# Recurrent stage: the sum of r times k moved into two 64x64 quadrants beside the variance product

## What is computed

```python
y = moveaxis(scan(step, S0, (r, w, k, v, kk, a)))            # the recurrence
mean = jnp.mean(y, axis=-1, keepdims=True)
var = jnp.mean(jnp.square(y - mean), axis=-1, keepdims=True)
y = (y - mean) * lax.rsqrt(var + GN_EPS)
y = y * gn_gain + gn_bias
y = y + jnp.sum(r * k * r_k, axis=-1, keepdims=True) * v     # the sum of r times k
y = y.reshape(bsz, seq, A_WIDTH).astype(dt) * jax.nn.silu(z)
```

## Time and profile before

| | |
|---|---|
| median of 3 runs | 2566.21 us (2562.79 to 2568.52) |
| profiled execution | 2567.88 us |
| its span on the core | 2566.1 us |
| mean granted clock | 0.998 |
| PE busy over the span | 2509.3 us, 98% |
| DVE, ACT, POOL busy | 54%, 31%, 46% |

### The profile page before, as it was taken

How to read it: one execution, slowest core, us unless ns; L and a number is a source line. 1 busy time by engine, 2 the same in 40 slices (tenths; PEclk the granted TensorE clock), 3 DMA queues, 4 the chain that set the end, 5 groups by cost and what they waited for, 6 DMA issues and landing times.

```text
span 2566.1 us, 52423 instructions
## 1 busy us (share of the span) xinstructions
PE 2509.3 (98%) x21640; PEld 2000.4 (78%) x21640; DVE 1382.1 (54%) x1496; ACT 804.2 (31%) x1187; POOL 1184.6 (46%) x1403
## 2 busy tenths in 40 slices
PE   8999999999999999999999999999999999999999
PEld 6777778888878888888888877777777777776877
DVE  7664431114676666652245675553647575654873
ACT  4433330002443333331013435554232323223241
POOL 7643324446676566565576651122422232323450
PEclk9999999999999999999999999999999999999999
DMA  3111001113222222273112220001111111114341
GB/s 141 42 34 34 26 26 49 49 49 115 107 74 90 74 82 90 76 267 115 49 49 82 82 74 18 16 16 68 44 37 55 40 56 39 39 64 165 140 139 58
DMA packets 46996, 184.25 MB, mean 72 GB/s; under 512 B 6257, under 2 KB 6769, under 8 KB 42609
## 3 DMA queue, kind: packets, MB, share of 16 engines
q1 hardware_dynamic: 30240, 106.01, 12.4%
q10 hardware_dynamic: 16592, 75.77, 7.7%
HBM read 145.06 MB, written 36.70 MB: 71 GB/s over the span
## 4 chain that ended last, share of the span: by engine, by line
PE 86%; DVE 7%; ACT 3%; issue 2%; DMA 1%; POOL 1%; ACTq 0%; POOLq 0%; DVEq 0%; SPq 0%
PE dps L336 36%; PE dps L354 14%; PE dps L1193 11%; PE aps L2519 6%; PE aps L1193 4%; PE aps L3389 2%; PE dps L697 2%; PE dps L688 1%; PE aps L675 1%; PE dps L1963 1%; PE aps L2055 1%; PE aps L2025 1%; PE dps L2076 1%; PE dps L2068 1%; DVE h_lo L404 1%
## 5 line engine op out<-in xcount | busy, mean ns | idle before, releaser
L3572 POOL TENSOR_TENSOR w_hi<-w_raw,one 128x256 fp32r<-128x256 f32 (+1 forms) x534 | 374.6, 731 | 1127.7 <-PE dps L336 514.0
L3577 POOL TENSOR_TENSOR w_lo<-w_raw,w_hi 128x256 fp32r<-128x256 f32 (+1 forms) x542 | 512.5, 975 | 13.3 <-ACT w_hi L1561 12.8
L336 PE MATMUL dps<-h_hi,w_hi 128*128 128x512 f32 x832 | 266.1, 395 | 12.8 <-POOL w_lo L3577 11.1
L1193 PE MATMUL dps<-op,ff_w 128*128 128x512 f32 x1122 | 270.1, 390 | 0.6 <-DVE op L1018 0.5
L336 PE MATMUL dps<-h_lo,w_hi 128*128 128x512 f32 x832 | 262.4, 390 | 0.0
L336 PE MATMUL dps<-h_hi,w_lo 128*128 128x512 f32 x832 | 262.3, 390 | 0.0
L1193 PEld LDWEIGHTS dps<-op,ff_w 128*128 128x128 f32 x1122 | 210.2, 188 | 46.3 <-DVE op L1018 2.1
L336 PEld LDWEIGHTS dps<-h_hi,w_hi 128*128 128x128 f32 x832 | 156.3, 189 | 50.7 <-POOL w_lo L3577 11.1
L336 PEld LDWEIGHTS dps<-h_lo,w_hi 128*128 128x128 f32 x832 | 156.9, 189 | 32.8
L336 PEld LDWEIGHTS dps<-h_hi,w_lo 128*128 128x128 f32 x832 | 156.7, 188 | 32.9
L336 PE MATMUL dps<-hid,w_hi 128*128 128x512 f32 x676 | 180.8, 389 | 1.1 <-DVEq L1460 1.1
(11 more groups left out here) (570 smaller groups left out, 4848.8 us busy)
## 6 DMA issues: line engine op xcount, KB each, us to landing
w_raw<-w_stream SPq DMA_DIRECT2D x192, 512.0 KB, 3.5
hid_t<-ff_up ACTq DMA_DIRECT2D x11, 1024.0 KB, 3.9
hid_raw<-hid_t ACTq DMA_DIRECT2D x22, 512.0 KB, 6.4
gates<-gate_out ACTq DMA_DIRECT2D x16, 512.0 KB, 3.3
gate_ring<-gates ACTq DMA_DIRECT2D x14, 512.0 KB, 4.8
x_res<-x_t ACTq DMA_DIRECT2D x2, 2048.0 KB, 7.8
x_res<-x_t ACTq DMA_DIRECT2D x4, 1024.0 KB, 6.0
x_t<-x_res ACTq DMA_DIRECT2D x4, 1024.0 KB, 4.1
```

The costliest lines, as they stand in the source:

```text
L336: mm = k.nc.tensor.matmul(k.dps[0:rows, pair, h * HALF:(h + 1) * HALF], w[:, slot, sub + t, 0:rows], x(t)[:, h * HALF:(h + 1) * HALF], sta ...
L1193: mm = k.nc.tensor.matmul(out, w[:, q, :], x, start=q == 0 and n == 0 and j not in (3, 5), stop=q == QUARTER - 1 and n == 2, skip_group_ch ...
L3572: g.tensor_tensor(k.w_hi[:, s, at], k.w_raw[:, s, at], ones, ALU.mult).then_inc(k.sem("w_hi_done"), 1)
L3577: return g.tensor_tensor(k.w_lo[:, s, at], k.w_raw[:, s, at], k.w_hi[:, s, at].bitcast(F32), ALU.subtract)
```

## The change

`rk` leaves level 4. At level 5, behind the wait for t5, one wide run of four 64x64 quadrant products of 512 columns takes the place of the variance product: for each head h, the variance from rows h to outputs h in bank 3, and `rk` from rows h to the other head's outputs in bank 2. The first half of the stage has no earlier half, so there only the two `rk` quadrants run. ScalarE gets a step `crossed`: two copies of 64x512 that put the halves of `rk` back in place in `rw_rk`, behind `std` and ahead of the `akv` copy. VectorE's multiplication by v moves from level 4 to behind the last level, ahead of the `rk_t` mask, and reads `rw_rk`. TensorE waits for the copy before it writes bank 2 again (w1 and rk_t). Level 4 now waits for the t4 mask. In the last half `back_load` moves from behind the `kq_tm` copy to behind the `w1` copy.

```diff
--- before.py
+++ after.py
@@ -281,6 +281,7 @@
         k.half[name] = k.half[room]
     for n, name in enumerate(("turn", "s", "y")):
         k.half[name] = k.at(f"rw_{name}", L + 2 * n * kb, [NC, HD])
+    k.rw_rk = k.at("rw_rk", L + 10 * kb, [HALF])
 
     k.back = [k.at(f"back{n}", at, [S]) for n, at in enumerate([X + 4 * n * kb for n in (0, 1, 2, 5, 6)] + [C, C + 4 * kb])]
     k.yb2_hi, k.yb2_lo, k.ya2_hi, k.ya2_lo = (k.at(name, H + 16 * n * kb, [PAIRS, S], F32R)
@@ -2283,10 +2284,10 @@
 EXPS = Steps("rw_exps", ["pc", "p", "q"])
 
 PRODUCTS = Steps("rw_product", ["lt", "lt_x", "l", "t1", "ak_t", "x1", "xt1", "t2", "v_tm", "x2", "xt2", "t3", "rb_t", "x3", "xt3",
-                                "t4", "kq_tm", "rk", "x4", "xt4", "kkp_tm", "t5", "bq_tm", "xt5", "akv", "u0", "w1", "rk_t", "m", "r", "y0"])
+                                "t4", "kq_tm", "x4", "xt4", "kkp_tm", "t5", "bq_tm", "rk", "xt5", "akv", "u0", "w1", "rk_t", "m", "r", "y0"])
 VALUES = Steps("rw_value", ["lt", "x_part", "x0", "xt_part", "xt0", "t1", "ak_t", "x1", "xt1", "t2", "x2", "xt2", "t3", "rb_t", "x3", "xt3",
-                            "t4", "rk", "x4", "xt4", "t5", "xt5", "rk_t", "m", "r", "s_in"])
-COPIES = Steps("rw_copy", ["v_tm", "kq_tm", "kkp_tm", "bq_tm", "akv", "u0", "w1"])
+                            "t4", "x4", "xt4", "t5", "xt5", "rk", "rk_t", "m", "r", "s_in"])
+COPIES = Steps("rw_copy", ["v_tm", "kq_tm", "kkp_tm", "bq_tm", "rk", "akv", "u0", "w1"])
 
 STATES = Steps("rw_state", [f"s{c}" for c in range(NC)])
 STATE_VALUES = Steps("rw_state_value", [f"s{c}" for c in range(NC)])
@@ -2296,7 +2297,7 @@
 Y_COPIES = Steps("rw_y_copy", ["y", "sq", "std"])
 
 BANK = {"lt": 0, "lt_x": 1, "l": 2, "t1": 0, "ak_t": 2, "x1": 1, "xt1": 0, "t2": 2, "v_tm": 1, "x2": 0, "xt2": 2, "t3": 1, "rb_t": 0,
-        "x3": 2, "xt3": 1, "t4": 0, "kq_tm": 2, "rk": 1, "x4": 1, "xt4": 0, "kkp_tm": 2, "t5": 1, "bq_tm": 2, "xt5": 0, "akv": 1, "rk_t": 2,
+        "x3": 2, "xt3": 1, "t4": 0, "kq_tm": 2, "rk": 2, "x4": 1, "xt4": 0, "kkp_tm": 2, "t5": 1, "bq_tm": 2, "xt5": 0, "akv": 1, "rk_t": 2,
         "u0": 0, "w1": 1, "y0": 2, "m": 0, "r": 1, "n": 3, "y": 3}
 
 
@@ -2598,12 +2599,8 @@
         b.then_inc(product, 1)
         if l < LEVELS:
             state(before, 2 * l - 1)
-        if l == 4:
-            u.wait(pe, VALUES, "xt3")
-            u.wait(pe, AHEAD, "rk")
-            k.nc.tensor.matmul(bank(k, "rk"), const(k, "headsum"), flat(made["rkv"]), start=True, stop=True).then_inc(product, 1)
         fill((count.late if l == LEVELS else count.level) - 1)
-        u.wait(pe, VALUES, "rk" if l == 4 else f"t{l}")
+        u.wait(pe, VALUES, f"t{l}")
         if l == 4:
             u.wait(pe, COPIES, "kq_tm")
             if before is not None:
@@ -2612,8 +2609,18 @@
             state_wait(before, 2 * l)
         else:
             u.wait(pe, COPIES, "bq_tm")
+            u.wait(pe, AHEAD, "rk")
             if before is not None:
-                rw_result_pe(k, pe, before, "var")
+                before.wait(pe, Y_COPIES, "sq")
+            for h in range(2):
+                if before is not None:
+                    var = k.nc.tensor.matmul(bank(k, "y")[HEADS[h]], const(k, "headsum")[HEADS[h], HEADS[h]], k.rw_out[HEADS[h], before.g, :],
+                                             start=True, stop=True, skip_group_check=True)
+                rk = k.nc.tensor.matmul(bank(k, "rk")[OTHER[h]], const(k, "headsum")[HEADS[h], HEADS[h]], flat(made["rkv"])[HEADS[h]],
+                                        start=True, stop=True, skip_group_check=True)
+            if before is not None:
+                var.then_inc(k.sem("rw_y_product"), 1)
+            rk.then_inc(product, 1)
         fill(1)
         if l < LEVELS:
             for c in range(NC):
@@ -2647,6 +2654,7 @@
         a = mul(bank(k, "u0"), SAME, c, other("xt"), other("akv"))
         mul(bank(k, "n"), HEADS, c, same("kq_tm"), same("v_tm"), start=c == 0, stop=False)
     a.then_inc(product, 1)
+    u.wait(pe, COPIES, "rk")
     for c in range(NC):
         a = mul(bank(k, "w1"), SAME, c, other("xt"), other("kkp_tm"))
         b = mul(bank(k, "rk_t"), SAME, c, channel("kq"), channel("rp"))
@@ -2909,10 +2917,6 @@
             rw_state_dve(k, dve, before, 2 * l - 1)
         elif before is not None:
             rw_result_dve(k, dve, before, "centred")
-        if l == 4:
-            rkv = flat(k.ahead["rkv"][u.g])
-            u.wait(dve, PRODUCTS, "rk")
-            v.tensor_tensor(rkv, bank(k, "rk"), k.rw_v[:, u.tokens], ALU.mult).then_inc(made, 1)
         steps(f"t{l}")
         for n, out in (("x", "xm"), ("xt", "xt")):
             if (n, l) != ("x", LEVELS):
@@ -2923,6 +2927,8 @@
         if l < 4:
             rw_state_dve(k, dve, before, 2 * l)
         steps(f"x{l}")
+    u.wait(dve, COPIES, "rk")
+    v.tensor_tensor(flat(k.ahead["rkv"][u.g]), k.rw_rk[:, :], k.rw_v[:, u.tokens], ALU.mult).then_inc(made, 1)
     u.wait(dve, PRODUCTS, "rk_t")
     mask("arkt", "rk_t", "incl_t").then_inc(made, 1)
     steps("ends")
@@ -3088,6 +3094,12 @@
         if u is not None:
             rw_result_act(k, act, u, step)
 
+    def crossed(u):
+        u.wait(act, PRODUCTS, "rk")
+        for to, src in zip(SAME, OTHER):
+            copied = a.activation(k.rw_rk[to, :], bank(k, "rk")[src], ACT.Copy)
+        copied.then_inc(k.sem("rw_copy"), 1)
+
     def spill(u):
         if u is not None:
             rw_spill(k, act, u, branches)
@@ -3103,6 +3115,7 @@
     copy(first, "bq_tm")
     result(prior[1], "sq")
     result(prior[1], "std")
+    crossed(first)
     copy(first, "akv")
     copy(first, "u0", -1.0)
     copy(first, "w1", -1.0)
@@ -3134,6 +3147,7 @@
         result(first, "sq")
         rw_shift_act(k, act, "r", i + 1, spilled)
         result(first, "std")
+        crossed(last)
         copy(last, "akv")
         copy(last, "u0", -1.0)
         copy(last, "w1", -1.0)
@@ -3144,15 +3158,16 @@
         spill(prior[1])
         gate(LAST_GATES[i][0], f"v{i}")
         copy(last, "kq_tm")
-        back_load(k, act, last, branches)
         copy(last, "kkp_tm")
         copy(last, "bq_tm")
         result(first, "sq")
         result(first, "std")
+        crossed(last)
         copy(last, "akv")
         gate(LAST_GATES[i][1], f"v{i}")
         copy(last, "u0", -1.0)
         copy(last, "w1", -1.0)
+        back_load(k, act, last, branches)
         result(last, "y")
         act.wait_ge(k.sem("gate_spilled"), 16 * (LAST_GATES[PAIRS - 1][1] + 1))
         for g in range(2):
```

## The result

The changed kernel takes 2570.39 us in the median (20 runs, 2568.74 to 2574.33), against 2566.19 us (20 runs) for the kernel before on the same chip: ratio 1.0019, 95% interval 1.0013 to 1.0025. It is 4.2 us slower where 3.0 us less was forecast: a miss of 7.2 us, outside the range. Against the bound of 0.2% the time counts as no change (it would begin at 2571.3), but the interval excludes a gain.

A forecast was written before the change was run, and what follows sets the result against it. The recurrent stage was taken as bound by TensorE's instruction list; seven halves at -3.4 us together and +0.4 for the first gave -3.0, other terms costing 0, so 2566.21 became 2563.2 us, range 2559.5 to 2567.5.

The forecast's parts named there:

- the price of the edit: TensorE, eight halves: rk removed saves 0.86 us each, wide run adds 0.38 in seven, 1.24 in the first; total -3.0 us.
- The wide run: TensorE at level 5: four quadrant products take 1.07 us, 1.79 us from filler to the first 64x64 matmul after.
- the two bunches that were named: Level 5: the wide run's eight matmuls start in two bunches of four, some 0.43 to 0.53 us apart.
- the two rivals on the array: Wide run: quadrants exclude each other on a bank, 2570.1 us, chance 0.06; all four run in a row, 2582.1, chance 0.02.
- levels and copies: Level 4's wait for the t4 mask, ScalarE's two added copies and VectorE's moved multiplication: each covered, cost 0.
- the issue waits: TensorE in the recurrent stage: three waits with no releaser, 2.5 us together, carried unchanged in the sum.
- The sum: TensorE's terms in the stage: -3.4 us for seven halves, +0.4 for the first, in all -3.0 us.
- the rival that named them: TensorE's issue waits, 2.5 us, may go, or the wide run is entered free: 2560.7 us or lower, chance 0.12.
- the seven DMA issues: Last half, back_load on ScalarE: moved issues take 3.38 us with 1.9 us of room, cost 0.
- the gate tile's landing: First gate tile, queued behind the branch loads: lands at 2351.6 to 2351.9 us, room 0.6 us or more, cost 0.
- a cover is lost: Gate tile lands 1 to 4 us late, or the akv copy is awaited: +1 to +4, 2564 to 2567 us, chance 0.12.

The follow-up runs named there:

- 8: The changed kernel run again unaltered, on the chip of the runs with waits at the head: 2571.09 us, ratio 1.0023 to the kernel before.
- 5: The changed kernel with 160 waits on an already set semaphore at the head of TensorE's program, shifting the stage by 80 instructions: 2563.63 us, ratio 0.9990.
- 3: The kernel before with eight dummy transposes (64 TensorE instructions) ahead of the stage's first product: 2570.61 us, ratio 1.0021.
- experiment 1: The kernel before with only the seven branch loads moved behind the w1 copy of the last half: 2567.84 us, ratio 1.0008.
- 9: The changed kernel with 244 waits on a set semaphore at the head of TensorE's program, a shift of 122 instructions: 2566.51 us, ratio 1.0002.
- 10: The changed kernel with 312 waits on a set semaphore at the head of TensorE's program, a shift of 156 instructions: 2567.94 us, ratio 1.0010.
- 4: The changed kernel with ten dummy transposes ahead of the stage's first product, a shift of 80 instructions: 2562.74 us, ratio 0.9993.
- experiment 2: The changed kernel with the branch loads issued later, behind the loads of the first two gate tiles: 2566.23 us, ratio 1.0006.

## Why the prediction was wrong, point by point

**Right: the price of the edit.** Level 4 (TensorE timeline of after, columns as in the earlier trace rows):

```profile
1977.79 0.73 PE L355 MATMUL dps<-h_hi,w_lo 128*128 128x512 f32 x2
1978.35 0.62 PE L355 MATMUL dps<-h_hi,w_hi 128*128 128x512 f32 x2
```

The headsum product is gone and the third filler starts 0.56 us after the first; 0.57 was forecast. The wide run:

```profile
1923.12 0.40 PE L355 MATMUL dps<-h_hi,w_lo 128*128 128x512 f32 x1
1923.44 0.64 PE L2617 MATMUL aps<-rw_out,const 64*64 64x512 f32 x1
1923.45 0.64 PE L2619 MATMUL aps<-rw_rkv,const 64*64 64x512 f32 x1
1923.46 0.64 PE L2617 MATMUL aps<-rw_out,const 64*64 64x512 f32 x1
1923.46 0.64 PE L2619 MATMUL aps<-rw_rkv,const 64*64 64x512 f32 x1
1923.92 0.59 PE L2617 MATMUL aps<-rw_out,const 64*64 64x512 f32 x1
...
1924.46 0.50 PE L355 MATMUL dps<-h_hi,w_lo 128*128 128x512 f32 x1
1924.89 0.27 PE L2520 MATMUL aps<-rw_xt,rw_t 64*64 64x64 f32 x2
```

Four start within 0.02 us, the next four 0.48 us later: the two bunches that were named. From the filler to the first 64x64 matmul it is 1.77 us (forecast 1.79), the run itself 1.02 (1.07). A half gains 0.44 to 0.65 us (0.48), half 1 loses 0.34 (0.38), and the eight together gain 3.2 (3.0). This also drops the two rivals on the array: quadrants of different row halves wrote one bank side by side. The Trainium skill, page TensorEngine Tiling (Array Packing), section Restrictions and Gotchas, forbids different row tiles one PSUM bank at the same time; this trace shows them there together, on different partitions, at 512 columns each with no time lost, and the measurement decides.

**Right: levels and copies.** No wait for the `rk` value, for `akv` or for the `rk_t` mask appeared. The `akv` copy starts 1.85 us behind the root instead of 1.37, 0.5 us late where 0.4 was forecast (ScalarE timeline of after):

```profile
2123.56 0.60 ACT L3205 ACTIVATE rw_rstd<-aps 128x512 f32<-128x512 f32 x1 [0.54 <-PE aps L2617]
2124.18 1.19 ACT L3100 ACTIVATE rw_rk<-aps 64x512 f32<-64x512 f32 x2
2125.41 0.60 ACT L3091 ACTIVATE rw_akv<-aps 128x512 f32<-128x512 f32 x1
```

**Wrong, and the main step: the issue waits.** The prediction had their row, saw that they "fall inside a series of matmuls with nothing to wait for" and that "the program's instructions shift", and drew from it only that "they may go". The sum carried them at no change, and the rival that named them had one sign. They could as well grow, and they grew from 2.5 to 8.7 us. The trace of before had what was needed to see it: the page lists the instruction queue, its three waits stand at one instruction number modulo 256 (92 or 93), and each ends just after a packet has landed. What an edit does to the places of the later series is countable before it is run, here 8 instructions more in each half. This step, with the lower clock that follows two of the waits, is the miss: a shift alone moved the changed kernel by 7.5 us (8 to 5), and one with 0.9 us of dummies the kernel before by 5.2 us upwards (3). The lower clock was in both profiles of the changed kernel and in no other version of it between 2280 and 2360 us; that it comes from the waits is inferred from that, and not shown by itself.

**Wrong in size: the seven DMA issues.** They were costed at nothing, with 0.6 us of room at the first gate tile. They hold ScalarE 5.01 us in place of 3.38. The term that was mis-sized is the gate tile's landing: forecast at 2351.6 to 2351.9, and in experiment 1 issued at 2344.36 and landed 9.9 us later, at 2354.2. Where no long issue wait had already made the chain later, it is late for VectorE four times out of five: by 1.12, 0.20, 1.05 and 0.91 us in experiments 1, 5, 9 and 10, and not in 4.

```profile
2336.62 5.01 ACTq L3230 DMA_DIRECT2D back<-branches  x7
```

The rival "a cover is lost" (+1 to +4) had this right, with a chance of 0.12. What no case had is the second cost of the loads, to the fetch of TensorE's program: in after it turns a wait of 1.2 us into one of 3.7, and without the loads the lower clock is gone too (experiment 2, -4.2 us against the first median of after, or -3.4 when each is taken against the kernel before beside it).

**The range.** Its lower side was set by a gain from the issue waits, its upper side by the late tile; the mechanism that decided had a price on one side only. The forecast of 2563.2 us is near what experiments 4 and 5 measure (2562.74 and 2563.63), but that is luck, misses against each other: they have less issue wait than was assumed (0.7 and 1.0 us for 2.5), while 4 pays for its dummies and 5 has the late tile.

## What to carry to other kernels

An "issue" wait inside a dense run of small matmuls can be program that has not arrived; see whether a packet of the instruction queue landed just before its end, and whether such waits stand at one instruction number modulo 256. If they do, that number is the block boundary, and where each dense run lies against it can be counted before and after an edit. An edit worth a few us can be judged only with the places held or tried at two or three shifts, since its own shift can cost or give more than it does; compare the stage with such waits taken off. And a block of loads moved ahead of a dense run competes with more than the transfers that it is queued with: it can also delay the fetch of the program.

## What the runs showed of the hardware

- TensorE's program came in packets of 16.4 KB, 256 instructions; each took 1.0 us in the median (0.9 to 2.2), and where TensorE waited it went on 1.2 to 1.6 us after the packet had landed. Successive packets around a wait of a dense series started 3.6 to 3.7 us apart in halves 1, 5 and 7 of after and 3.3 in half 8 of experiment 2, and 6.0 us with the loads at 98.3% of the DMA engines' time.
- All 41 issue waits of the stage in thirteen traces stand at one instruction number modulo 256.
- 64x64 matmuls consumed 256 instructions in 2.3 us, less than the 3.3 us from one packet to the next; whether a series with two boundaries waited went with the start of the second block's packet, after TensorE had passed the first boundary (19 of 19) or before (0 of 11).
- Four 64x64 quadrants with 512 columns, two banks, both row halves on one bank, ran side by side: 1.02 us for the two passes of an f32 product, against 1.06 us for a pair.
- A wait of 1.74 us was followed by 3.4 us at the lower clock level and one of 3.67 us by 6.8 us; one of 1.72 us at 2341.21 and one of 2.00 us in experiment 3 were not followed by any.
- Waits on a set semaphore are not free at the head of the program: with 160 TensorE started at 11.1 us as without (11.1 in before), with 192 at 11.5, with 244 at 14.2 and with 312 at 17.8: the last 68 waits took 3.7 us, 54 ns for one.
